# Gate matrices by indirect adding transfers from GpSimd instead of one-hot products, and 52 pairs of expert rows in seven products instead of 40

## The reference, cut to what matters

```python
q = (xb @ peer_wq).reshape(PEER_BLOCK, PEER_HEADS, 2, PEER_QDIM // 2)
s = jnp.einsum('bhpd,hpnd->bhpn', q, peer_keys)
sv, si = lax.top_k(s, PEER_TOPK)
cand = sv[:, :, 0, :, None] + sv[:, :, 1, None, :]
sc, flat = lax.top_k(cand.reshape(...), PEER_TOPK)
e = i1 * N_KEYS + i2
gate = jax.nn.softmax(sc, axis=-1)
h = jax.nn.gelu(jnp.einsum('bhkd,bd->bhk', peer_u[e], xb))
return jnp.einsum('bhk,bhkd->bd', gate * h, peer_v[e])
```

## Time and profile before

| | us |
|---|---|
| median of 3 runs | 5859.01 |
| lowest and highest | 5856.02, 5861.28 |
| span of the profiled execution, first to last instruction | 5850.3 |

### The profile page before, as it was taken

How to read it: one execution, slowest core, us unless ns; L and a number is a source line. 1 busy time by engine, 2 the same in 40 slices (tenths; PEclk the granted TensorE clock), 3 DMA queues, 4 the chain that set the end, 5 groups by cost and what they waited for, 6 DMA issues and landing times. The chain is left out here.

```text
span 5850.3 us, 112850 instructions
## 1 busy us (share of the span) xinstructions
PE 5750.6 (98%) x48619; PEld 5594.9 (96%) x48619; DVE 3821.5 (65%) x4806; ACT 2286.9 (39%) x2840; POOL 490.7 (8%) x324
## 2 busy tenths in 40 slices
PE   8999999999999999989999999999999999999999
PEld 7888889999999999989999999999999999999998
DVE  5565653232357533267876687777778888889898
ACT  4333322222233322122234443333335556555655
POOL 1000000000000000000026651111110000000000
PEclk9999999999999999999999999999999999999999
DMA  3111113232223433221334445555554333335642
GB/s 103 45 44 47 43 55 126 88 110 88 107 98 126 155 125 138 90 97 69 107 117 160 160 158 150 149 148 146 150 149 168 130 120 110 141 119 144 176 125 85
DMA packets 374407, 682.04 MB, mean 117 GB/s; under 512 B 219616, under 2 KB 234976, under 8 KB 346464
## 3 DMA queue, kind: packets, MB, share of 16 engines
q1 hardware_dynamic: 366928, 656.81, 34.1%
q10 hardware_dynamic: 7056, 19.00, 0.8%
HBM read 562.37 MB, written 113.37 MB: 116 GB/s over the span
## 5 line engine op out<-in xcount | busy, mean ns | idle before, releaser
L2755 PE MATMUL ps<-va_h_high,va_v_high 128*128 128x288 f32 x3584 | 1056.2, 295 | 10.5 <-DVE va_h_low L140 7.6
L2757 PE MATMUL ps<-va_h_high,va_v_low 128*128 128x288 f32 x3584 | 1057.6, 295 | 0.0
L2756 PE MATMUL ps<-va_h_low,va_v_high 128*128 128x288 f32 x3584 | 1056.5, 295 | 0.0
L2755 PEld LDWEIGHTS ps<-va_h_high,va_v_high 128*128 128x128 f32 x3584 | 673.4, 188 | 11.3 <-DVE va_v_low L140 7.8
L2757 PEld LDWEIGHTS ps<-va_h_high,va_v_low 128*128 128x128 f32 x3584 | 673.3, 188 | 0.0
L2756 PEld LDWEIGHTS ps<-va_h_low,va_v_high 128*128 128x128 f32 x3584 | 673.3, 188 | 0.0
L140 DVE TENSOR_TENSOR ah_ul<-ah_u,ah_uh 128x1024 fp32r<-128x1024 f32 (+1 forms) x288 | 435.1, 1511 | 212.3 <-ACT ah_uh L2309 161.1
L140 DVE TENSOR_TENSOR rwkv_wl<-ret_w,rwkv_wh 128x2048 fp32r<-128x2048 f32 (+1 forms) x137 | 258.5, 1887 | 375.0 <-ACT rwkv_wh L1270 312.1
L1165 PE MATMUL ps<-rwkv_hn_high,rwkv_wh 128*128 128x288 f32 x1632 | 479.4, 309 | 0.6 <-PEq L225 0.6
L1166 PE MATMUL ps<-hn_low,rwkv_wh 128*128 128x288 f32 x1632 | 455.3, 294 | 0.0
L2135 PE MATMUL ps<-hn_high,ah_uh 128*128 128x288 f32 x1536 | 431.3, 297 | 4.9 <-DVE ah_ul L140 4.8
(11 more groups left out here) (493 smaller groups left out, 14853.7 us busy)
## 6 DMA issues: line engine op xcount, KB each, us to landing
va_v<-peer_v SPq DMA_DIRECT2D x96, 1024.0 KB, 5.4
ah_u<-peer_u SPq DMA_DIRECT2D x160, 512.0 KB, 6.5
ah_u<-peer_u SPq DMA_DIRECT2D x48, 1024.0 KB, 5.2
ret_w<-w_ret SPq DMA_DIRECT2D x46, 1024.0 KB, 4.8
h_kept<-ah_h SPq DMA_DIRECT2D x128, 288.0 KB, 2.3
gates<-ah_stage SPq DMA_DIRECT2D x12, 3072.0 KB, 9.6
ah_hidden<-h_kept SPq DMA_DIRECT2D x60, 576.0 KB, 5.0
ah_v<-peer_v SPq DMA_DIRECT2D x30, 1024.0 KB, 4.9
```

The source lines that it names most:

```text
L2755: pe.matmul(z, ah[:, r, f], th[:, q, r, :], start=begin, stop=False, skip_group_check=True)
L2756: pe.matmul(z, ah[:, r, f], tl[:, q, r, :], start=False, stop=False, skip_group_check=True)
L2757: done = pe.matmul(z, al[:, r, f], th[:, q, r, :], start=False, stop=r == R - 1, skip_group_check=True)
```

## The change

The gate matrices are no longer made by products. POOL clears a DRAM tensor `gate_rows` (128 rows x 128 experts x 576 tokens) during `out_stage`. In `gates_stage` DVE computes, for each token tile and each of its 128 slots (8 heads x 16), the address of the cell (expert, token), and POOL issues one indirect DMA per slot, which adds the 128 gates of that slot (one per token, 4 bytes each) into 128 cells: 640 in all. The 16 of one head must have landed before the next head's go out for the same token tile; the tiles 1 and 2, and 3 and 4, take turns. The `middle` segment is gone, so 24 rows are made one by one and 104 in 52 pairs. The rows 24 to 79 (the 28 pairs below `UNWEIGHED`) are stored without their gates and are multiplied in `finish_stage`, which begins with row 80. SP waits for all 640 before it loads the gates of pair 28. POOL makes `alone` before its transfers, and DVE makes the low part of `t3` in POOL's place.

```diff
@@ out_stage
+        nothing = sb("zeros", [P, HT])
+        K.gate_rows = nc.dram_tensor("gate_rows", (ROWS, P, T), F32, kind="Internal").ap()
...
+        @block.gpsimd
+        def _(pool):
+            pool.memset(nothing[:, :], 0.0).then_inc(blank, 1)
+            pool.wait_ge(blank, 1)
+            for r in range(ROWS):
+                pool.wait_ge(made, 1 + 3 * r // 4)
+                pool.dma_start(K.gate_rows[r].rearrange("p (h t) -> p h t", h=2),
+                               nothing[:, :].unsqueeze(1).broadcast_to([P, 2, HT])).then_inc(cleared, 16)
+            pool.wait_ge(cleared, 16 * ROWS)
@@ gates_stage
-    MIDDLE = EARLY + 2 * NST
-    PLAIN = MIDDLE + 4
+    PLAIN = EARLY + 4
     PAIRED = (ROWS - PLAIN) // 2
+    WEIGHED = 80
+    UNWEIGHED = (WEIGHED - PLAIN) // 2
+    SLOTS = PH * TOPK
...
-        K.weighed_from = PLAIN
+        K.weighed_from = WEIGHED
...
+        cell = K.gate_rows.rearrange("r p (t o) -> (r p t) o", o=1)
...
             def gates(p, s):
-                sp.dma_start(gate[s][:, :].rearrange("p (s t) -> p s t", t=TC), K.gates[:, :, PLAIN + 2 * p + s, :])\
-                    .then_inc(gate_in[s], 16)
+                if (p, s) == (UNWEIGHED, 1):
+                    for n in range(NTT):
+                        sp.wait_ge(scattered[n], 16 * SLOTS)
+                sp.dma_start(gate[s][:, :], K.gate_rows[PLAIN + 2 * p + s]).then_inc(gate_in[s], 16)

             def keep(p, s):
-                sp.wait_ge(weighed, 2 * p + 2 - s)
+                if p < UNWEIGHED:
+                    sp.wait_ge(gelu, PLAIN + 2 + 2 * p + 2 - s)
+                else:
+                    sp.wait_ge(weighed, 2 * (p - UNWEIGHED) + 2 - s)
                 sp.dma_start(K.h[PLAIN + 2 * p + s], hs[:, s, :]).then_inc(kept[s], 16)
...
                 for s in (1, 0):
                     keep(p, s)
-                    if p + 1 < PAIRED:
+                    if UNWEIGHED <= p + 1 < PAIRED:
                         gates(p + 1, s)
...
-            def middle(s, k):
-                for g in range(3):
-                    n = 12 * s + 3 * k + g
-                    pe.wait_ge(rowed, n + 1)
-                    pe.wait_ge(moved, n + 1)
-                    for t in range(4):
-                        last = pe.matmul(X[g][:, P * t:P * t + P], hot[:, 1, 4 * g + t, :], rows[:, 4 * g + t, :],
-                                         start=True, stop=True)
...
         @block.gpsimd
-            with pool.Fori(0, NST) as s:
...
+            pool.wait_ge(v_s.sem, v_s.of(PH - 1, "1"))
             pool.tensor_tensor(alone[:, :, :], b22[0].bitcast(F32), b12[0].bitcast(F32), ALU.subtract)
...
-            pool.wait_ge(t_high, 3)
-            pool.tensor_tensor(t3[1], alone[:, :, :], t3[0].bitcast(F32), ALU.subtract).then_inc(lone, 1)
-            for p in range(PAIRED - 1):
+
+            def scatter(n, h):
+                m = P if n < NTT - 1 else TS
+                if h:
+                    pool.wait_ge(scattered[n], 16 * TOPK * h)
+                for k in range(TOPK * h, TOPK * h + TOPK):
+                    pool.indirect_dma_start(cell, bass.IndirectOffsetOnAxis(ap=cells[0:m, n, k:k + 1], axis=0),
+                                            shares[0:m, n, k:k + 1], None, compute_op=ALU.add)\
+                        .then_inc(scattered[n], 16)
+
+            pool.wait_ge(ided, 1)
+            for h in range(PH):
+                scatter(0, h)
+            for n in (1, 3):
+                pool.wait_ge(ided, n + 2)
+                for h in range(PH):
+                    scatter(n, h)
+                    scatter(n + 1, h)
+            for p in range(UNWEIGHED, PAIRED - 1):
                 for s in (1, 0):
                     weigh(pool, p, s)
...
@@ gates_stage, DVE, at the end of a token tile's routing
+                    dve.tensor_tensor(shares[:, i, :].rearrange("p (h k) -> p h k", h=PH), gate,
+                                      total[:, :].unsqueeze(2).broadcast_to([P, PH, TOPK]), ALU.mult)
+                    dve.scalar_tensor_tensor(out=expert[:, :, :], in0=ids[:, 0, :, :], scalar=float(NK),
+                                             in1=ids[:, 1, :, :], op0=ALU.mult, op1=ALU.add)
                     dve.drain()
+                    dve.scalar_tensor_tensor(out=cells[:, i, :].rearrange("p (h k) -> p h k", h=PH),
+                                             in0=expert[:, :, :], scalar=float(T),
+                                             in1=token[:, :].unsqueeze(2).broadcast_to([P, PH, TOPK]),
+                                             op0=ALU.mult, op1=ALU.add).then_inc(ided, 1)
+                    dve.drain()
+                    dve.tensor_scalar(token[:, :], token[:, :], float(P), None, ALU.add)
+                    dve.drain()
...
+            dve.wait_ge(t_high, 3)
+            low(dve, t3[1], alone[:, :, :], t3[0]).then_inc(lone, 1)
@@ finish_stage: the gates of four rows in one transfer
             def gates(g_, s, k):
-                for r in (2 * s, 2 * s + 1):
-                    sp.dma_start(g[:, r, :].rearrange("p (s t) -> p s t", t=TC),
-                                 K.gates[:, :, row(g_) + 2 * r + k, :]).then_inc(hg_in[k], 16)
+                src = K.gate_rows[row(g_) + 4 * s:row(g_) + 4 * s + 4].rearrange("(r k) p t -> k p r t", k=2)[k]
+                sp.dma_start(g[:, 2 * s:2 * s + 2, :], src).then_inc(hg_in[k], 16)
```

More of the change, by code:

```diff
@@ L1944, in gates_stage @@
         few, base = over("few", [P, TOPK], base)
[L1945 to L1949, removed]
+        expert, base = over("expert", [P, PH, TOPK], base)
+        token, base = over("token", [P, 1], base)
         assert base <= keys_at
@@ L1990, in gates_stage @@
         consts = sem("consts")
-        diff, exped, ided, turned, slotted = sem("diff"), sem("exp"), sem("ids"), sem("turned"), sem("slots")
-        hotted, rowed, gated, moved = sem("hot"), sem("rows"), sem("gates"), sem("staged")
-        stored = sem("stage_stored")
+        diff, exped, ided = sem("diff"), sem("exp"), sem("ids")
+        scattered = [sem(f"gates_scattered{n}") for n in range(NTT)]
         chained, lone, t_high, t_low = sem("chain_sum"), sem("lone_sum_and_low"), sem("t_high"), sem("t_low")
@@ L2017, in bank, with segments @@
             return K.ps[:, (j + 4) % 8, 0:HT]
-        def segments(eng, tile, early, middle, late=1):
+        def segments(eng, tile, early, late=1):
             if late:
@@ L2026, in segments @@
                     early(i, k)
[L2027 to L2031, removed]
         def nothing(i, k):
@@ L2065, in tile @@
                 sp.dma_start(K.h[t], hs[:, s, :]).then_inc(kept[s], 16)
-            def middle(s, k):
[L2068 to L2072, removed]
+            segments(sp, tile, nothing)
             def part(p, n):
@@ L2098, in _ @@
                 part(1, n)
-            for s in (1, 0):
-                gates(0, s)
             for p in range(PAIRED):
@@ L2127, in _, with tile @@
         def _(pe):
-            def tile(t, s, more, between=None):
+            def tile(t, s, more):
                 pe.wait_ge(lowered, t + 1)
@@ L2200, in _ @@
                 route(i, False)
[L2201 to L2211, removed]
+            segments(pe, tile, nothing)
+            for t in range(EARLY + 1, PLAIN):
                 tile(t, t % 2, False)
@@ L2293, in early @@
                     act.activation(ids[:, 2, :, :], ids[:, 2, :, :], ACT.Exp).then_inc(exped, 1)
[L2294 to L2306, removed]
+            segments(act, tile, early)
             def high(j, source):
@@ L2486, in early @@
                     dve.drain()
-                    dve.tensor_tensor(gate, gate, total[:, :].unsqueeze(2).broadcast_to([P, PH, TOPK]), ALU.mult)\
-                        .then_inc(ided, 1)
+                    dve.tensor_tensor(shares[:, i, :].rearrange("p (h k) -> p h k", h=PH), gate,
+                                      total[:, :].unsqueeze(2).broadcast_to([P, PH, TOPK]), ALU.mult)
+                    dve.scalar_tensor_tensor(out=expert[:, :, :], in0=ids[:, 0, :, :], scalar=float(NK),
+                                             in1=ids[:, 1, :, :], op0=ALU.mult, op1=ALU.add)
                     dve.drain()
-            def middle(s, k):
-                if k == 0:
-                    dve.wait_ge(slotted, NTT + 1)
-                for g in range(3):
-                    t = slice(4 * g, 4 * g + 4)
-                    dve.wait_ge(gated, 12 * s + 3 * k + g + 1)
-                    dve.tensor_tensor(hot[:, :, t, :], iota[:, :].unsqueeze(1).unsqueeze(1).broadcast_to([P, 2, 4, P]),
-                                      slots[:, 0:2, bass.ds(TC * s + 12 * k + 4 * g, 4)].unsqueeze(3)
-                                      .broadcast_to([P, 2, 4, P]), ALU.is_equal).then_inc(hotted, 1)
-            segments(dve, tile, early, middle, 0)
+                    dve.scalar_tensor_tensor(out=cells[:, i, :].rearrange("p (h k) -> p h k", h=PH),
[5 more added lines that the diff above has]
```

(2 more changed lines are left out.)

57 lines of the change are left out of this document (17 added, 40 removed).

## The result

The changed kernel takes **6144.68 us** (median of 4 runs, 6140.39 to 6148.57) against 5860.15 us (4 runs, 5856.02 to 5863.24) for the kernel before on the same chip: a ratio of 1.048, 95% interval 1.047 to 1.049. The forecast was 5685 us. The profiled execution took 6147.73 us, its span is 6145.9.

What follows compares the result with a forecast made beforehand. PE was taken to bound the kernel (98% busy). Savings of 165.0 + 6.6 + 4.8 less 2 for clearing made 174.4 us, so 5859.01 became 5685 us; range 5672 to 5850, likeliest case 5672 to 5705.

Steps and rivals of the forecast that it cites:

- the price of an adding transfer: POOL's 640 indirect transfers in the gates stage: 1.1 us each, ending at 3525, 160 us early.
- My bounds: Limits for one indirect transfer: 0.55 us, SP's issue of a gate load, to 1.8 us, the smallest transfer's landing.
- the deadline of 1.35: Highest price per transfer, 1.35 us, at which all 640 fit between 2806 and 3687, before PE stands still.
- in time: Likeliest case: the transfers land before SP's wait costs PE anything; 5685 us, own range 5672 to 5705; chance 0.64.
- rival 4: Transfers so late that the kernel is slower, above 1.62 us each; at 1.8 us, 288 late, 5973 us; chance 0.12.
- Pairs in place of the middle segment: 12 more pairs, 268.4 us, replace the 433.4 us of 24 rows with gate matrices: 165.0 us saved.
- Transposes: Among the single rows, three transposes per turn of four rows go: 1.3 us a turn, 6.6 us saved.
- The passage: From single rows to pairs, PE's two waits for a low part go as `alone` is made earlier: 4.8 us saved.
- Clearing: POOL's 128 stores of 288 KB during the output stage: cost 0 to 10 us of late weights, 2 taken.
- The last stage: At the kernel's end, DVE multiplies four more groups of eight rows with gates: cost 0, up to 24 us if uncovered.
- DVE beside the transfers: While POOL issues, DVE may be held up; nothing lost up to 0.2 us per issue, 0 us taken.
- rival 3: POOL's issues hold DVE; at 0.62 us each, 262 us of PE waiting, 5947 us; chance 0.07.

Runs made afterwards that it cites:

- copy_not_add: The changed kernel with its 640 indirect transfers overwriting their cells instead of adding to them: 5837.2 us (one run).
- no_transfers: The changed kernel with all 640 adding transfers left out, SP waiting for the routing instead: 5693.3 us, ratio 0.971 to the kernel before.
- clearing_alone: The kernel before with only the clearing of `gate_rows` added to `out_stage`, the cleared tensor unused: 5867.2 us, ratio 1.0007.

## Why the prediction was wrong, by its steps

**The step that failed: the price of an adding transfer**, "I take 1.1 us, near the middle". It measured 2.08, from the start of one transfer to the next. What it is made of, from the runs (512 transfers have 128 addresses, 128 have 64, so the undisturbed adding issue is 0.8 x 1.55 + 0.2 x 1.42 = 1.52 on the mean):

| part | us each | from |
|---|---|---|
| a copying issue, mean of 128 and 64 addresses | 0.95 | copy_not_add: 0.96 and 0.89 |
| adding | 0.57 | 1.55 and 1.42 against those |
| gap behind each issue | 0.31 | 198.3 / 640 |
| behind DVE's two-input instructions | 0.22 | the mean issue, 1.739, less 1.52 |
| waiting between the heads of tile 0 | 0.03 | 19.5 / 640 |
| sum | 2.08 | |

The 1.1 was near the price of a copy that nothing disturbs (0.95 + 0.31 = 1.26, which would have been in time; beside the pairs even copies came to 1.58 and were late). The two terms that decide weren't in it at all: what the adding costs the issuer, 368 us over 640, and DVE's instructions, 138 us. My bounds, 0.55 to 1.8 us, were of transfers from SP's queue and left both out, so even the upper one was too low. With no row of the kind in the trace, the price was anyone's between the bounds, and the deadline of 1.35 lay inside them; a chance of 0.64 for "in time" rested on a middle value alone, and the stated range, 5672 to 5850, left out every case in which it fails by much.

The Trainium skill (DMA: Bandwidth & Descriptors, Latency and other measured facts) puts the emission of a GpSimd-issued transfer at about 1 us. The copying issues agree (0.96); the adding ones don't (1.55), and the gap and DVE come on top.

**The mechanism of the loss was right**: rival 4 (0.12), with the deadline and the order of the stand as worked out. SP came to its wait at 3691 where I had 3674, and PE stopped at 3713 where I had 3687 (the pairs began at 3060.6 instead of 3041.5: the single rows began 12 us later than before, and 5 are the wait of the passage, below). The 12 us are not shown to be the change's: in the profile of no_transfers, which clears as well, they began only 1 us later than before (2743.1 against 2741.9), and it and the changed kernel are already 11.5 us apart when the first clearing store starts (1708.6 and 1720.1). The first transfer moved by 19 us too (2825 instead of 2806), so the break-even price stayed near 1.35. From where PE stopped, each microsecond was lost in full. Its price was worked out at 1.8 us, 5973; at 2.08 the same sum gives 640 x 0.73 = 467 late, 6152, and the time was 6145. It decides from 1.62 us, and 2.08 is well beyond.

**Pairs in place of the middle segment, 165.0: right.** 52 pairs took 1162.6 us (22.36 each, 22.37 taken).

**Transposes, 6.6: right.** From gelu to gelu a turn of four single rows is 49.92 us now (2825.16 to 2875.08), against 51.16, which gives 6.2 in five turns.

**The passage, 4.8: wrong by its whole size.** The waits of the earlier trace rows are gone, but `alone` collides with DVE at its new place too:

```profile
2770.97 7.17 DVE L140 TENSOR_TENSOR ah_ul<-ah_u,ah_uh 128x2048 fp32r<-128x2048 f32 x1 [0.28 <-issue]
2778.06 7.26 DVE L2412 TENSOR_TENSOR ah_cand<-top_v 128x2048 f32 x1
```

```profile
2776.13 7.04 POOL L2322 TENSOR_TENSOR ah_alone<-ah_alone,hn_low 128x2304 f32<-128x2304 f32 x1
2783.32 7.05 POOL L2324 TENSOR_TENSOR ah_alone<-ah_alone,hn_low 128x2304 f32<-128x2304 f32 x1
```

DVE is held in two instructions in a row, some 10 us together if 2.29 us is taken as the undisturbed length of either (the shortest of L2412 takes 2.28), and PE waits 5.2 us for a low part (no_transfers has the same wait). So PE's lead here was about 5 us, not the 25 of two rows that I had counted on.

**Clearing, 2: held.** clearing_alone leaves between 1 us less and 10 us more.

**The last stage, 0: held.** It takes 1461 us (4684.6 to the end) against 1460 before (4390.2 to the end), with the gates of ten groups on DVE in place of six.

**DVE beside the transfers, 0 lost: right, and rival 3 fell.** The contention that it was about is there, but the other way round: POOL's issues wait for DVE, which the prediction priced nowhere.

Together: without the transfers the change gives 5693.3 against 5863.3, 170 us less, where 174.4 were forecast; the 4.8 of the passage are about the difference. The rest of the error, some 450 us, is one term.

## What to carry to other kernels

Work that moves to an engine with "room" gets a deadline, and its price has to be known as well as the deadline is: work out the price at which it breaks even (here 1.35 and 1.62 us), and where bounds lie on both sides of it, forecast with the chances that they give and not with the middle. Count for an indirect transfer that POOL issues the issuer's whole turn (issue, gap, and the reduction, if it adds), not the landing. And if such transfers are late, first fill them (128 addresses in each), then copy where nothing has to be added yet, and move the wait behind more work that doesn't need them.

## What the runs showed of the hardware

- Adding instead of copying lengthens the *issue* of an indirect transfer on POOL from 0.96 to 1.55 us (128 cells of 4 bytes); 64 addresses in place of 128 save only 0.07 us (copy) to 0.13 us (add).
- An issue waits for a DVE instruction with two SBUF inputs that is already running (up to 1.0 us for one of 1.22 us); in step with the pairs this makes ten issues to each 22.36 us. DVE doesn't wait for issues (1226 ns with them and without).
- In the hole PE's granted clock was at the lower of its two levels, 1.2 GHz: 0.50 in the window of 3723 to 4157, in which PE did nothing, and full again soon after PE went on, as the windows show:

```profile
4157.00:4182.00 25.00, 18.91 (x122) 18.91 (x123) 18.54 (x20) 6.54 (x9) 3.43 (x2) 0.76 0.70 222
4182.00:4300.00 118.00, 118.00 (x889) 118.00 (x888) 92.34 (x100) 46.24 (x53) 17.19 (x10) 1.00 0.46 146
```
